# Three-pass value products in the memory attentions of a two-block transformer: rounded part and rest, scale in the queries, row maximum written negated

## What is computed

```python
def memory_cross_attention(h, m, wq, wkv, wo):
    b, t, _ = h.shape
    q = (h @ wq).reshape(b, t, XA_HEADS, XA_HEAD_DIM)        # 4 heads of 256
    k, v = jnp.split(m @ wkv, 2, axis=-1)
    k = k.reshape(b, MEM_LEN, XA_HEADS, XA_HEAD_DIM)
    v = v.reshape(b, MEM_LEN, XA_HEADS, XA_HEAD_DIM)
    s = jnp.einsum("bthd,bmhd->bhtm", q, k).astype(jnp.float32) * (XA_HEAD_DIM ** -0.5)
    p = jax.nn.softmax(s, axis=-1).astype(v.dtype)
    o = jnp.einsum("bhtm,bmhd->bthd", p, v).reshape(b, t, D_MODEL)
    return o @ wo
```

## Time and profile before

| what | value |
|---|---|
| three runs | 2378.35, 2384.07, 2384.29 us, median 2384.07 |
| profiled execution | 2382.32 us, its span 2380.5 us |
| busy share PE / weight loads / DVE / ACT / POOL | 99 / 78 / 51 / 39 / 42 % |
| granted clock of PE | 0.998 of full speed |
| first memory attention (scores to values) | 499.4 to 532.0 us of the span |
| second and third | from 1186.14 and from 1935.08 us |

### The profile page before, as it was taken

The page is one execution under the profiler, slowest core; times in us unless marked ns, Lnnn a source line. Parts: engine busy times, 40 slices in busy tenths (PEclk is TensorE's granted clock), DMA queues, the critical chain, the costliest instruction groups (busy, mean ns, idle before and its releaser), DMA issues.

```text
span 2380.5 us, 29353 instructions
## 1 busy us (share of the span) xinstructions
PE 2346.3 (99%) x10890; PEld 1862.0 (78%) x10890; DVE 1219.1 (51%) x2026; ACT 939.4 (39%) x1418; POOL 997.8 (42%) x744
## 2 busy tenths in 40 slices
PE   8999999999999999999999999999999999999999
PEld 6777778878888888757878888887667877888887
DVE  4454546244433436794457555546774243655544
ACT  3345444334222227524444222225875443322222
POOL 4323335223544545635425545444123233545443
PEclk9999999999999999999999999999999999999999
DMA  5222222422223223222213232232013421332231
GB/s 174 71 72 93 91 89 89 160 71 93 98 97 106 88 92 104 89 71 94 84 58 106 89 106 88 90 104 77 29 36 101 166 71 64 105 100 95 88 106 71
DMA packets 170087, 218.71 MB, mean 92 GB/s; under 512 B 6584, under 2 KB 144106, under 8 KB 169974
## 3 DMA queue, kind: packets, MB, share of 16 engines
q1 hardware_dynamic: 168278, 214.59, 27.5%
q10 hardware_dynamic: 1696, 2.61, 0.3%
HBM read 215.05 MB, written 2.12 MB: 91 GB/s over the span
## 4 chain that ended last, share of the span: by engine, by line
PE 89%; DVE 4%; ACT 3%; issue 1%; POOL 1%; DMA 1%; SPq 0%; DVEq 0%; ACTq 0%
PE ps_l L964 79%; PE ps_l L1388 2%; PE ps_l L1113 1%; PE ps_s L1371 1%; POOL w_lo L810 1%; ACT w_hi L1633 1%; PE ps_s L1475 1%; DVE small L3030 1%; DVE arena L3022 1%; PE ps_s L1490 1%; PE ps_s L1265 0%; PE ps_s L1312 0%; PE ps_s L964 0%; DVE small L3032 0%; PE ps_l L1248 0%
## 5 line engine op out<-in xcount | busy, mean ns | idle before, releaser
L810 POOL TENSOR_TENSOR w_lo<-w_raw,w_hi 128x512 fp32r<-128x512 f32 (+1 forms) x740 | 997.6, 1380 | 1361.5 <-ACT w_hi L1633 1342.9
L964 PE MATMUL ps_l<-a_hi,w_hi 128*128 128x512 f32 x1936 | 763.5, 394 | 3.8 <-POOL w_lo L810 2.7
L964 PE MATMUL ps_l<-a_lo,w_hi 128*128 128x512 f32 x1952 | 758.9, 389 | 0.0
L964 PE MATMUL ps_l<-a_hi,w_lo 128*128 128x512 f32 x1936 | 754.5, 390 | 0.0
L1633 ACT ACTIVATE w_hi<-w_raw 128x2048 fp32r<-128x2048 f32 (+2 forms) x196 | 370.6, 1891 | 596.9 <-PE ps_l L964 578.4
L964 PEld LDWEIGHTS ps_l<-a_hi,w_hi 128*128 128x128 f32 x1936 | 363.0, 187 | 90.0 <-issue 9.6
L964 PEld LDWEIGHTS ps_l<-a_lo,w_hi 128*128 128x128 f32 x1952 | 366.2, 188 | 78.6 <-issue 3.1
L964 PEld LDWEIGHTS ps_l<-a_hi,w_lo 128*128 128x128 f32 x1936 | 363.0, 187 | 77.3
L964 PE MATMUL ps_l<-b_hi,w_hi 128*128 128x512 f32 (+1 forms) x892 | 330.1, 370 | 6.0 <-issue 2.3
L964 PE MATMUL ps_l<-b_hi,w_lo 128*128 128x512 f32 (+1 forms) x892 | 327.2, 367 | 0.0
L964 PE MATMUL ps_l<-b_lo,w_hi 128*128 128x512 f32 (+1 forms) x892 | 327.1, 367 | 0.0
(11 more groups left out here) (308 smaller groups left out, 2414.6 us busy)
## 6 DMA issues: line engine op xcount, KB each, us to landing
w_raw<-in_ffn_w_up_dram SPq DMA_DIRECT2D x44, 1024.0 KB, 5.1
w_raw<-in_w_dram SPq DMA_DIRECT2D x32, 1024.0 KB, 5.2
w_raw<-in_ffn_w_down_dram SPq DMA_DIRECT2D x22, 1024.0 KB, 4.8
w_raw<-in_w_in_dram SPq DMA_DIRECT2D x20, 1024.0 KB, 5.4
w_raw<-in_xa_wkv_dram SPq DMA_DIRECT2D x16, 1024.0 KB, 5.2
w_raw<-in_w_kv_mem_dram SPq DMA_DIRECT2D x8, 1024.0 KB, 5.3
w_raw<-in_xa_wq_dram SPq DMA_DIRECT2D x8, 1024.0 KB, 4.9
w_raw<-in_xa_wo_dram SPq DMA_DIRECT2D x8, 1024.0 KB, 5.0
```

The costliest lines, as they stand in the source:

```text
L810: e.tensor_tensor(w_lo[:, b % 2, o], w_raw[:, b % 2, o], w_hi[:, b % 2, o].bitcast(F32), ALU.subtract).then_inc(w_lo_made[by], 1)
L964: ins = pe.matmul(o, *((v, w) if swap else (w, v)), start=first and n == 0, stop=last and n == 2)
```

## The change

The memory attentions' value products go through `mm3` too. For that the memory's values are kept as `VM_hi` (written by ACT) and `VM_lo` (written by DVE in `value_rest`), and the turned probabilities as a rounded part, written by ACT, and a rest, written by DVE (`turned_rest`, which waits for ACT's part), in the buffers `A2_hi` and `A2_lo`, a separate pair of tiles per head. In both places it is now DVE that frees the PSUM bank ("vv" and `t_who="v"` in the plan). Apart from this the scale of 1/16 goes into the eviction of the queries, and `reduce_max(..., negate=True)` writes the negated maximum directly, so that the small operation behind it is gone.

```diff
     def values(c, wkv, j):
-        L.add(f"xv{c}{j}", "aa")
+        L.add(f"xv{c}{j}", "vv")
...
-        attention(f"xa{c}", XA_HEADS, 3, "a", 1, after=(2, 2, 3, 3, 3), halves=(0, 2))
+        attention(f"xa{c}", XA_HEADS, 3, "a", 1, t_who="v", after=(2, 2, 3, 3, 3), halves=(0, 2))
...
+        VM_lo = sb("vm_lo", [P, 2, D], FR)
...
+        VM_hi = sb("vm_hi", [P, 2, D], FR)
...
         def ptx(h):
-            return ar(1024 + 1024 * (h % 2), MT, T)
+
+            return A2_hi[:, MT * h:MT * (h + 1), :], A2_lo[:, MT * h:MT * (h + 1), :]
...
+                    o = slice(h * 256 + d * P, h * 256 + (d + 1) * P)
+                    ph, pl = ptx(h)
                     for m in range(MT):
-                        ins = pe.matmul(bank(L, g)[:, :], vM[:, m, h * 256 + d * P:h * 256 + (d + 1) * P],
-                                        ptx(h)[:, m, :], start=m == 0, stop=m == MT - 1)
+                        ins = mm3(bank(L, g)[:, :], VM_hi[:, m, o], VM_lo[:, m, o], ph[:, m, :], pl[:, m, :],
+                                  m == 0, m == MT - 1)
...
-                        act.activation(vM[:, t, 512 * v:512 * v + 512], bank(L, g + t)[:, :], ACT.Copy)\
-                            .then_inc(l_free["a"], 1)
+                        act.activation(VM_hi[:, t, 512 * v:512 * v + 512], bank(L, g + t)[:, :], ACT.Copy)\
+                            .then_inc(vm_hi, 1)
...
-                def copy(g, h, i):
+                def turned_hi(g, h, i):
+                    wait_group(act, L, g)
                     tiles = bank(L, g)[:, 0:MEM].rearrange("p (m q) -> p m q", q=P)
-                    act.activation(ptx(h)[:, :, i * P:(i + 1) * P], tiles, ACT.Copy).then_inc(l_free["a"], 1)
-                copy_turned = copies_of_turned(f"xa{c}", copy)
+                    act.activation(ptx(h)[0][:, :, i * P:(i + 1) * P], tiles, ACT.Copy).then_inc(t_hi, 1)
...
-                                       scale=1 / 16, accum_out=ls[:, u % 8:u % 8 + 1]).then_inc(s_free["a"], 1)
+                                       accum_out=ls[:, u % 8:u % 8 + 1]).then_inc(s_free["a"], 1)
...
+                    if kind == "T" and turned:
+                        turned(g, h, i)
                     if kind == "P":
                         values(g, h, i)
...
+            def value_rest(c, v):
+
+                for t in range(MT):
+                    wait_group(dve, L, L.base[f"xv{c}{v}"] + t)
+                    dve.wait_ge(vm_hi, 2 * MT * c + MT * v + t + 1)
+                    o = slice(512 * v, 512 * v + 512)
+                    dve.tensor_tensor(VM_lo[:, t, o], bank(L, L.base[f"xv{c}{v}"] + t)[:, :],
+                                      VM_hi[:, t, o].bitcast(F32), ALU.subtract).then_inc(l_free["v"], 1)
...
                     low_part(dve, b)
                     low_part(dve, b + 1)
+                    value_rest(c, 0)
+                    value_rest(c, 1)
                 dve.wait_ge(n_rstd, k_norm + 1)
-                scaled(L.base[f"xq{c}"], 8, lambda j: qT[:, j, :])
+                for j in range(KD):
+                    g = L.base[f"xq{c}"] + j
+                    wait_group(dve, L, g)
+                    dve.scalar_tensor_tensor(out=qT[:, j, :], in0=bank(L, g)[:, :], scalar=1 / 16, in1=rst,
+                                             op0=ALU.mult, op1=ALU.mult).then_inc(l_free["v"], 1)
...
                     wait_group(dve, S, g)
-                    step(dve.reduce_max(mx[:, u % 8:u % 8 + 1], bank(S, g)[:, 0:MEM], AX_X))
-                    sync()
-                    dve.tensor_scalar(nm[:, u % 8:u % 8 + 1], mx[:, u % 8:u % 8 + 1], -1 / 16, None, ALU.mult)\
+                    dve.reduce_max(nm[:, u % 8:u % 8 + 1], bank(S, g)[:, 0:MEM], AX_X, negate=True)\
                         .then_inc(u_nm, 1)
...
+                def turned_rest(g, h, i):
+                    wait_group(dve, L, g)
+                    dve.wait_ge(t_hi, TT * (XA_HEADS * c + h) + i + 1)
+                    tiles = bank(L, g)[:, 0:MEM].rearrange("p (m q) -> p m q", q=P)
+                    ph, pl = ptx(h)
+                    o = slice(i * P, (i + 1) * P)
+                    dve.tensor_tensor(pl[:, :, o], tiles, ph[:, :, o].bitcast(F32), ALU.subtract)\
+                        .then_inc(l_free["v"], 1)
...
+            value_rest(1, 0)
             wait_read(dve, L, L.base["pc_out_a"] + 7)
+            value_rest(1, 1)
             residual(L.base["pc_out_b"], 5)
```

More of the change, by code:

```diff
@@ L561, in build @@
             pass
-        sb("arena_low_half", [P, HALF])
+        sb("arena_low", [P, 1536])
+        VM_lo = sb("vm_lo", [P, 2, D], FR)
+        sb("arena_mid", [P, 10752 - 3584])
+        VM_hi = sb("vm_hi", [P, 2, D], FR)
+        sb("arena_high", [P, HALF - 12800])
         A2_hi, A2_lo = sb("a2_hi", [P, KD, T], FR), sb("a2_lo", [P, KD, T], FR)
@@ L656, in build @@
         bf_col = sb("forget_bias", [8, 1])[:, :]
-        kT, qT, vM = ar(4096, 8, MEM), ar(R0, 8, T), ar(10752, 2, D)
+        kT, qT = ar(4096, 8, MEM), ar(R0, 8, T)
         mem_st = [ar(o, 2, D) for o in (2560, 10752, R0)]
@@ L724, in build @@
         o_hi = sem("o_hi")
+        t_hi, vm_hi = sem("turned_hi"), sem("memory_values_hi")
         sub_sq, sub_rs, sub_n, sub_lo = sem("sub_sq"), sem("sub_rs"), sem("sub_n"), sem("sub_lo")
@@ L1959, in cross @@
                         act.activation(p_x[:, i, :], bank(S, g)[:, 0:MEM], ACT.Exp, bias=nm[:, u % 8:u % 8 + 1],
-                                       scale=1 / 16, accum_out=ls[:, u % 8:u % 8 + 1]).then_inc(s_free["a"], 1)
+                                       accum_out=ls[:, u % 8:u % 8 + 1]).then_inc(s_free["a"], 1)
                     if kind == "T":
-                        copy_turned(g, h, i)
+                        turned_hi(g, h, i)
                     if kind == "O":
@@ L2465, in plain_norm, with walk @@
                     .then_inc(u_p, 1)
-            def walk(name, heads, scores, exp_done, buf, width, values, filled=None):
+            def walk(name, heads, scores, exp_done, buf, width, values, filled=None, turned=None):
                 ev, at = plan.events[name]
@@ L2678, in values @@
                                       A_hi[:, 2 * h + d, :].bitcast(F32), ALU.subtract).then_inc(l_free["v"], 1)
-                walk(name, XA_HEADS, scores, lambda h, i: wait_read(dve, S, at["S", h, i]), p_x, lambda i: MEM, values)
+                def turned_rest(g, h, i):
[6 more added lines that the diff above has]
+                        .then_inc(l_free["v"], 1)
+                walk(name, XA_HEADS, scores, lambda h, i: wait_read(dve, S, at["S", h, i]), p_x, lambda i: MEM, values,
+                     turned=turned_rest)
                 residual(L.base[f"xo{c}"], after, *([angle_steps()] if c == 1 else []))
```

## The result

The changed kernel takes 2385.20 us (median of 12 runs, 2382.25 to 2386.66), where the kernel before takes 2381.35 (12 runs on the same chip, 2378.06 to 2384.29). The ratio is 1.0017, with a 95% interval of 1.0009 to 1.0025: slower, by 3.9 us, where a gain of 2.2 us was forecast. That is inside the stated range (2374 to 2389), but on the other side of the kernel before. The profiled execution took 2383.48 us.

What follows compares the result with a forecast made beforehand. PE was taken as the bound, with DVE pacing each attention's first phase. Cheaper value products (8.6 us at most), less the DVE-ACT loop's cost, left 2.2 us gained: 2382.3 to 2380.1, given as 2381, range 2374 to 2389.

Steps and rivals of the forecast that it cites:

- the walk: Step-by-step timing of the first memory attention: end at 531.3 instead of 532.0, 0.7 us gained per attention, 2.2 in all.
- the sum: Whole kernel: profiled 2382.3 us less 2.2 is 2380.1; by the median 2381.9; 2381 given.
- The loop: DVE and ACT in each attention: from step 3 each step is one round through both, 1.66 us against 0.99 to 1.27.
- Maximum 3: Row maximum of score tile 3, first attention: starts at 504.26 - 0.19 = 504.07, the small DVE operation being gone.
- Five steps at 1.66: First attention, steps 3 to 8: maximum 8 at 504.07 + 5 x 1.66 = 512.37, 2.6 us late.
- back 0.03: Handover from ACT's copy to DVE's turned rest within each round: 0.03 us of the 1.66.
- The pairs behind: Pairs of steps with one value group, after step 9: PE needs 3.52 us against 3.89 before, DVE 3.41.
- The value products: On PE in the memory attentions: three rounded matmuls of 0.2273 us, 0.68 a product instead of 0.86; at most 8.6 us saved.
- The turned rest: New DVE subtraction per turned tile, 48 operations of 128x256 from PSUM: 0.42 us each, priced like the row maximum.
- the second rival: Turned rest on DVE takes 0.69 us, so DVE bounds each attention: 7.5 us slower, 2389.8; chance 0.12.
- The first rival: The DVE-ACT loop in the attentions costs nothing, the whole 8.6 us is gained: 2373.7; chance 0.13.
- The memory's values: Splitting their four 128x512 pieces per attention adds four DVE operations of 0.69 us, hidden before the query projection: costed at nothing.

Runs made afterwards that it cites:

- the copy ahead: Changed kernel, but ACT copies the turned tile of three steps earlier before the current tile's exponentials: 2378.01 us, ratio 0.9982 to the kernel before.
- the transposes: 32 small transposes of a constant added at PE's start: kernel before 2382.86 us (1.0006), changed kernel 2382.82 (1.0004), changed kernel with ACT's copy before exponentials 2375.47 (0.9974).
- the rest held back: Changed kernel, with DVE making the rest of a turned tile one step later, behind the next maximum: 2388.12 us, ratio 1.0033 to the kernel before.

## Why the prediction was wrong, point by point

The forecast was 2.2 us less and the result 3.9 us more, an error of some 6 us. The attentions make 2.8 of it, in four terms of the walk; the rest is the load ahead of the third attention and the clock behind it, for which the sum had no term.

**The loop** was described rightly: DVE waits before each turned rest for ACT's copy, its maxima go from 1.0 to 1.27 us apart to 1.74, and PE's first value group waits for a bank. What failed are four terms of the walk, each small, all of one sign. The times are from the attention's start, forecast and measured. Maximum 3: 504.07 - 499.40 = 4.67, measured 503.28 - 498.42 = 4.86; the 0.19 us for the removed small operation were booked in a stretch where POOL sets the pace, and are nothing there. Five steps at 1.66 were 1.73 on average (511.93 for maximum 8, or 13.51; forecast 12.97): the term mis-sized is "back 0.03", the way from ACT's copy to DVE's rest, which is 0.10. I had taken the one way, from DVE to ACT, for both. The trace of the kernel before has the other way too, in its last stretch, where ACT's copy of a value product ends at 526.65 and DVE's rest starts at 526.75:

```profile
526.05 0.60 ACT L1965 ACTIVATE a_hi<-ps_l 128x512 fp32r<-128x512 f32 x1 [0.40 <-PE ps_l L1388]
...
526.75 0.69 DVE L2677 TENSOR_TENSOR a_lo<-ps_l,a_hi 128x512 fp32r<-128x512 f32 x1 [0.46 <-ACT a_hi L1965]
```

The pairs behind were 3.55 instead of 3.52. So tile 15's scores start at 24.07 instead of 23.45, 0.6 late. In the tail PE waits 0.31 us more ahead of the fifth value group, for the bank of the turned rest, which the walk did not have; the last three groups start 4.55 us behind tile 15 instead of 4.35, and take 4.20 instead of 4.09. Together 0.62 + 0.20 + 0.11 = 0.93 us per attention, 2.8 in all: from 2.2 gained to 0.6 lost.

**The value products** cost what was forecast: 0.23 us a matmul, with the first behind a float32 transpose 0.31 (513.91 to 514.23); the pair of steps confirms the sum.

**The turned rest** at 0.42 us, the price that decided between the forecast and the second rival, was right, and that rival is out. But it said of itself that 0.06 us per step take the gain away, and 0.07 per step is what the handover took. The number stood there; my own range gave it 0.05.

**The first rival** (the loop costs nothing) is out, and the experiment with the copy ahead shows what is there to be had once the loop does not hold: 1.95 us per attention against the changed kernel, 1.73 against the kernel before, where this rival had 2.9.

**The memory's values** were hidden, as costed: ahead of all three attentions the query projection is one unbroken piece of the chain, 144 matmuls in 32.69 us, 0.227 each, as in the kernel before.

**The sum** was "2382.3 us of the profiled execution less 2.2". The missing term is of another kind, in no attention: it comes from PE's longer list. From the ratios it is 1.0017 or 1.0014 less 1.0004, which is 2.4 to 3.1 us, by the changed kernel with and without the transposes; 0.9982 less 0.9974, 1.9 us, by the kernel with the copy ahead; 1.4 to 1.8 us by the kernel before. With the 0.6 us of the attentions this makes 2.0 to 3.7 of the 3.8 to 3.9 measured. Each ratio is uncertain by 0.0008 or 0.0009 and a difference of two by some 0.0012, which is about 3 us, so the medians alone barely show the term. The traces show it more sharply. From the issue of that load to the end of the span (of the first of before, 2380.5 - 1853.13) it is 527.3 to 527.4 us in the three traces of the kernel before and 527.5 in the changed kernel with the transposes, where the load is early; where it is late, it is 529.0, 531.5 and 530.9 us in the three of the changed kernel and 531.0 in the kernel before with the transposes. With the copy ahead it is 528.8 without the transposes and 525.5 with them. So the late load and what follows it cost 1.5 to 4 us, least in the trace whose clock stays full. The prediction counted PE's instructions by their time and never by their place in the list.

What is open: the transposes also shift every other packet of code by the same number of instructions, and it matters where in a load a packet falls. In the three kernels with transposes one lies 4.5 to 5.0 us behind the issue of the first load of a like pair, near 417 us, and that load takes 5.3 to 5.4 us (5.3 to 5.6 in the others); the second load of the pair takes 7.0 to 7.1 us there, and 5.8 to 6.8 in the ten without transposes. And stretches at the lower clock earlier in the program vary from trace to trace (of the kernel before, one has a granted clock of 0.86 over 1720 to 1732 us and again over 1788 to 1800, another 1.00 in both); the load near 1853 us is issued anywhere between 1849.82 and 1853.13 in the three traces of before. So how much of the 1.5 to 4 us a median shows is known only to some 2 us. Why the clock fell behind the late load in four traces and not in the other two is open as well. That the packet of code slows one of the 16 DMA engines, whose part of the load then lands last, fits the rows but was not shown. Why the first matmul of three passes behind a transpose costs 0.08 more was not tried.

## What to carry to other kernels

When a value is split in two by two engines, the second engine's part waits for the first's; look at what stands ahead of the first part on its engine, and put the copy before whatever waits for the second engine, so that no round trip forms inside a step. When such a round is priced, read each direction of the handover from rows of its own. An operation taken from an engine that shares its pace with another (here DVE beside POOL) gained nothing in that stretch, so its saving is counted by stretches and not by its number. And where the difference between two kernels is larger than the stage that was edited shows, align the two traces from the end: in a program this close to its bound, a transfer that lands 1.4 us later elsewhere costs more than the edit.

## What the runs showed of the hardware

Code is fetched while the kernel runs, in packets on queues of their own ("q8 instruction", 0.02 MB each in the rows), and such a packet 1.0 to 2.9 us behind the issue of a load of 1 MB, with a second one issued 2.15 us behind the first, went with a landing 1.4 to 2.4 us later (6.9 to 7.9 us instead of 5.3 to 5.5), in six traces of six; without it, in seven of seven, 5.3 to 5.5. At 4.5 to 5.0 us behind the issue it did not delay the first load of another such pair (5.3 to 5.4 us, three traces). The number of instructions ahead on PE decides where it falls: 32 matmuls and their weight loads at the very start moved it, in a kernel of 10938 matmuls. After the longer wait PE's granted clock was 0.83 on average from 1860 to 1870 us in four of the six (two of the changed kernel, the copy ahead, the kernel before with transposes) and full in the other two (one of the changed kernel, the rest held back); where it fell, the 53 matmuls behind took 8.64 us instead of 7.14 (second trace of the changed kernel), and the 1.5 us are about as much as the wait had added.

The handover between two engines is not the same both ways here: from the end of DVE's maximum to ACT's exponentials 0.04 us, from the end of ACT's copy to DVE's rest 0.10.

DVE's scaling of 128x256 from SBUF to SBUF takes 0.35 us alone and 0.84 beside POOL, 0.65 when it starts later in POOL's operation: beside POOL it ended 0.15 us behind the end of POOL's operation in both cases, so its end goes at POOL's pace of 1.27 us, whenever it starts.
